# Modulation vectors: one matmul against a table of identities after a block transpose and a VectorE sum, in place of four or eight matmuls against a column of ones

## The reference, cut to what matters

```python
mod = jax.nn.silu(c) @ w_ada[l] + b_ada[l]          # (1, 1024) @ (1024, 6144)
sh1, sc1, g1, sh2, sc2, g2 = jnp.split(mod, 6, axis=-1)
h = modulate(rms_norm(x, norm1_g[l]), sh1, sc1)      # h * (1 + sc1) + sh1
x = x + g1[:, None, :] * token_mixer(h, ...)
h = modulate(rms_norm(x, norm2_g[l]), sh2, sc2)
x = x + g2[:, None, :] * squared_relu_mlp(h, w_ff1[l], w_ff2[l])
```

## Time and profile before

| | |
|---|---|
| median of 3 runs | 3011.77 us (3007.27 to 3013.6) |
| profiled execution, span from first to last instruction | 3012.7 us |
| mean granted TensorE clock | 0.980 |
| PE busy / DVE busy / ACT busy | 2901.2 / 1681.3 / 996.1 us |
| matmuls of the 32 turns (L780) | 448 records |
| DVE additions of the slots (L1930) | 279.6 us busy |

### The profile page before, as it was taken

One profiled execution on the slowest core, in us unless ns is written; L12 is line 12 of the kernel. 1 busy time (PEld: TensorE's weight loads), 2 busy tenths in 40 slices (PEclk: granted clock), 3 DMA queues, 4 the chain that ended last, 5 costly groups with the idle time before them and its releaser, 6 DMA issues.

```text
span 3012.7 us, 39817 instructions
## 1 busy us (share of the span) xinstructions
PE 2901.2 (96%) x15873; PEld 2488.4 (83%) x15873; DVE 1681.3 (56%) x2278; ACT 996.1 (33%) x1374; POOL 117.7 (4%) x156
## 2 busy tenths in 40 slices
PE   6999999999999999999989999999999998999999
PEld 5888887979787888789878888888888987878887
DVE  5656655454555666665487555455555348554444
ACT  3333333232333222332275232122123336432222
POOL 0000000000001100000000000000000000000000
PEclk8999999999999999999989999999999999999999
DMA  6433344535333644333520213222322250222332
GB/s 227 130 118 123 110 148 136 177 109 154 93 119 103 193 129 142 100 111 125 126 54 18 84 43 91 85 88 88 105 78 72 83 112 29 71 73 87 98 104 70
DMA packets 267439, 316.91 MB, mean 105 GB/s; under 512 B 24811, under 2 KB 236155, under 8 KB 267292
## 3 DMA queue, kind: packets, MB, share of 16 engines
q1 hardware_dynamic: 241116, 230.74, 25.1%
q0 software_dynamic: 19456, 72.00, 7.8%
q10 hardware_dynamic: 6720, 12.06, 1.3%
HBM read 291.96 MB, written 11.27 MB: 101 GB/s over the span
## 4 chain that ended last, share of the span: by engine, by line
PE 85%; DVE 6%; ACT 3%; DVEq 3%; issue 2%; DMA 1%; SPq 0%; ACTq 0%
PE psum L611 25%; PE psum L613 24%; PE psum L612 24%; PE psum L1010 2%; PE psum L780 1%; PE psum L826 1%; PE psum L1022 1%; DVE n_t L1863 1%; DVE dneg L2373 1%; DMA ada<-in_w_ada 1%; DVE sba L2384 1%; PE psum L894 1%; DVE w_lo L1875 1%; PE psum L813 1%; ACT pt L1671 1%
## 5 line engine op out<-in xcount | busy, mean ns | idle before, releaser
L611 PE MATMUL psum<-hs_hi,w_hi 128*128 128x512 f32 x1632 | 652.9, 400 | 12.9 <-DVE hs_lo L1867 5.7
L1875 DVE TENSOR_TENSOR w_lo<-raw,w_hi 128x2048 fp32r<-128x2048 f32 (+1 forms) x246 | 435.4, 1770 | 395.9 <-ACT w_hi L1243 283.4
L612 PE MATMUL psum<-hs_hi,w_lo 128*128 128x512 f32 x1632 | 640.1, 392 | 0.0
L613 PE MATMUL psum<-hs_lo,w_hi 128*128 128x512 f32 x1632 | 639.8, 392 | 0.0
L611 PEld LDWEIGHTS psum<-hs_hi,w_hi 128*128 128x128 f32 x1632 | 309.7, 190 | 88.5 <-issue 15.2
L613 PEld LDWEIGHTS psum<-hs_lo,w_hi 128*128 128x128 f32 x1632 | 309.1, 189 | 66.2
L612 PEld LDWEIGHTS psum<-hs_hi,w_lo 128*128 128x128 f32 x1632 | 309.8, 190 | 63.7 <-issue 2.2
L1930 DVE SCALAR_TENSOR_TENSOR ada_acc<-ada_raw,csil,ada_acc 128x512 f32<-128x512 f32 x392 | 279.6, 749 | 48.8 <-DMA ada_raw<-in_w_ada 26.3
L1253 ACT CAST w_hi<-raw 128x2048 fp32r<-128x2048 f32 (+1 forms) x138 | 191.4, 1387 | 328.8 <-PE psum L613 296.0
L611 PE MATMUL psum<-mid_hi,w_hi 128*128 128x512 f32 x768 | 299.7, 390 | 0.0
L612 PE MATMUL psum<-mid_hi,w_lo 128*128 128x512 f32 x768 | 299.2, 390 | 0.0
(11 more groups left out here) (357 smaller groups left out, 4568.2 us busy)
## 6 DMA issues: line engine op xcount, KB each, us to landing
raw<-in_w_in SPq DMA_DIRECT2D x56, 1024.0 KB, 5.2
ada_raw<-in_ada_w POOLq DMA_DIRECT2D x96, 512.0 KB, 4.3
raw<-in_w_ff SPq DMA_DIRECT2D x48, 1024.0 KB, 5.6
raw<-in_w_ff SPq DMA_DIRECT2D x96, 512.0 KB, 3.4
ada_raw<-in_w_ada POOLq DMA_DIRECT2D x32, 512.0 KB, 4.7
raw<-in_w_in SPq DMA_DIRECT2D x24, 512.0 KB, 4.6
ada<-in_w_ada SPq DMA_DIRECT2D x4, 2048.0 KB, 18.6
raw<-in_w_ret_out SPq DMA_DIRECT2D x16, 512.0 KB, 3.5
```

The source lines that it names most:

```text
L611: pe.matmul(dst, lhi, rhi, start=start, stop=False)
L612: pe.matmul(dst, llo, rhi, start=False, stop=False)
L613: return pe.matmul(dst, lhi, rlo, start=False, stop=stop)
L1875: low = dve.tensor_tensor(w_lo[par][:, k0:kt], raw[par][:, k0:kt], w_hi[par][:, k0:kt].bitcast(F32), ALU.subtract)
```

## The change

`ada_acc` is no longer summed over the partitions by PE alone. At the end of the fourth slot of a group DVE transposes the accumulator in square blocks of 32 by 32 (into `ada_raw`, which is free by then) and sums each row of a block, which leaves 16 or 32 numbers on each partition. PE then multiplies them once with `fold`, a 128 by 128 table made of sixteen 32 by 32 identities, which adds the four groups of 32 partitions. The result has the wanted numbers of each quarter of the partitions in columns of its own, so a take now reads and writes 32 partitions at a time: four additions in place of one or two. `fold` is filled once, in the first head, by four copies. It lies where `vrow2` was.

```diff
             def ada_turn(g, par, vecs=1, bank_=C1):
                 pe.wait_ge(ada_sum, 4 * g + 4)
                 ...
-                for v in range(vecs):
-                    for b in range(4):
-                        mm = pe.matmul(bank_[:, 4 * v + b:4 * v + b + 1], ada_acc[par][:, v, b * P:(b + 1) * P], ones_c[:, 0:1],
-                                       start=True, stop=True)
-                mm.then_inc(ada_mm, 1)
+                pe.matmul(bank_[:, 0:16 * vecs], fold[:], ada_acc[par][:, 0, 0:16 * vecs], start=True, stop=True).then_inc(ada_mm, 1)
...
             def ada_slot(s, i=None, two=True):
                 ...
+                if kp == 3:
+                    vecs = 2 if two else 1
+                    turned = ada_raw[par][:, 0:vecs, :].rearrange("p v n -> p (v n)")
+                    dve.drain()
+                    dve.transpose(turned, acc[:, 0:vecs, :].rearrange("p v n -> p (v n)"))
+                    dve.drain()
+                    last = dve.tensor_reduce(acc[:, 0, 0:16 * vecs], turned.rearrange("p (b j) -> p b j", j=32), AX.X, ALU.add)
                 last.then_inc(ada_sum, 1)
 
+            def fold_table():
+                dve.wait_ge(v2_t, 1)
+                for a in range(4):
+                    r_ = slice(32 * a, 32 * a + 32)
+                    dve.tensor_copy(fold[r_, :].rearrange("p (q i) -> p q i", q=4), bc(ident[r_, r_], 4))
+
+            def quarter(bank_, q, vecs):
+                src = bank_[32 * q:32 * q + 32, 0:16 * vecs].rearrange("p (v c q) -> p v c q", v=vecs, q=4)[:, :, :, q]
+                return src if vecs > 1 else src[:, 0]
...
             def ada_take1(g):
                 dve.wait_ge(ada_mm, g + 1)
-                dve.tensor_tensor(mod1[:, bass.ds(16 + 4 * g, 4)], C1[:, 0:4], vec1[:, bass.ds(24 + 4 * g, 4)],
-                                  ALU.add).then_inc(ada_evac, 1)
+                for q in range(4):
+                    r_ = slice(32 * q, 32 * q + 32)
+                    last = dve.tensor_tensor(mod1[r_, bass.ds(16 + 4 * g, 4)], quarter(C1, q, 1), vec1[r_, bass.ds(24 + 4 * g, 4)], ALU.add)
+                last.then_inc(ada_evac, 1)
 
             def ada_take2(g, l):
                 ...
-                for v in range(2):
-                    last = dve.tensor_tensor(mod2[l][:, v, bass.ds(c0, 4)], (X1 if l else C1)[:, 4 * v:4 * v + 4],
-                                             vec2[:, l, bass.ds(c0, 4)], ALU.add)
+                for q in range(4):
+                    r_ = slice(32 * q, 32 * q + 32)
+                    last = dve.tensor_tensor(mod2[l][r_, :, bass.ds(c0, 4)], quarter(X1 if l else C1, q, 2),
+                                             bc(vec2[r_, l, bass.ds(c0, 4)], 2), ALU.add)
                 last.then_inc(ada_evac, 1)
```

More of the change, by code:

```diff
@@ L198, in build @@
         vrow2 = at("vrow2", [P, P], F32, o + 5120)
+        fold = at("fold", [P, P], F32, o + 5120)
         vrow3 = at("vrow3", [V3_ROWS, P], F32, o + 5632)
@@ L2043, in ret_head @@
                     dve.tensor_tensor(qk_raw[:, jb, 0:w], src[:, c0:c0 + w], decay[:, 0:w], ALU.mult).then_inc(s_masked, 1)
+                if not with_out:
+                    fold_table()
                 for s in range(2):
```

## The result

The changed kernel takes 2978.32 us (median of 4 runs, 2972.74 to 2978.58), the kernel before beside it 3011.51 us (3007.27 to 3013.6). That is 33 us less. The ratio of the two is 0.9883, with a 95% interval from 0.987 to 0.9897; 0.9883 of 3011.51 us are 2976.3 us. Forecast were 2987 us and a range from 2977 to 3001.

A forecast was written before the change was run, and what follows sets the result against it. PE, busy 96% of the span, was taken as the bound; 10.1 + 3.5 + 15.4 - 4.1 = 24.9 us off the profiled 3012.7 gave 2987.8, as a median 2987 us, range 2977 to 3001.

The forecast's parts named there:

- Prices of DVE: For 1024 numbers, transpose 1.22 us and sum about 1.22; a take's four additions between 0.36 and about 0.9 us.
- The rivals with a transpose of 2.4 to 6.7 us: Dearer transpose on DVE: two to four times, 2993 to 3006 us (22%), or 6.7 us, 3028 us (4%).
- slower: Rival: transpose at the reciprocal's rate, 6.7 us for 1024 numbers, makes the whole 3028 us; chance 4%.
- A new turn is 0.22 us: On PE, one float32 matmul per turn; saves 0.59 us at turns 0 to 7, 1.48 at 8 to 31.
- Heads: Turns 0 to 5: a loss of 4.1 us, from 0.6, 0.6, 2.3 and 0.6 for a lower-clock stretch.
- The shorter turn in front of L833 starts this chain 0.59 us earlier: Later heads: earlier chain against takes 2 x 0.6 longer, so PE comes out 0.6 us later each.
- D: What a group adds on DVE, transpose, sum and drains: 2.6 us with two vectors, 1.55 with one.
- First feed-forward: Turns 14 to 19: 3.5 us gained, 2.0 at turns 16 to 18, 1.5 at turn 19, none at 14 and 15.
- I count nothing for both: Turns 14 and 15, first feed-forward: no gain, since PE already waits 0.97 us for a weight late to ACT.
- I take half, 0.7 each: Turns 26 and 28, ends of a pass with context: PE idles for its branch, so 0.7 us each, 1.4 together.
- A branch that changes its length: Sign that the forecast is wrong: a loop's branch on PE or DVE changes its length; no size given.
- rival 2: DVE hides everything: up to all 40.2 us come out, 2972 us, more likely half way, 2980; chance 13%.

The follow-up runs named there:

- e3: Changed kernel with each take made as before, one or two additions over 128 partitions (results not the reference's): 2971.52 us.
- e12: Changed kernel without DVE's transpose and sum, takes over 128 partitions, 48 more PE instructions before the first loop (results not the reference's): 2970.40 us.
- e11: The kernel before, unchanged, run once more for a second trace: 3012.71 us.
- e7: The kernel before with 160 more instructions (waits long satisfied) on PE before its first loop: 3001.62 us.
- e8: Changed kernel with a group's four slots in the first feed-forward's loop moved to the first two units of each half pass: 2979.02 us.
- e5: Changed kernel with 48 more instructions (waits long satisfied) on PE before its first loop: 2969.61 us.
- e6: Changed kernel with 256 more instructions (waits long satisfied) on PE before its first loop: 2979.33 us.
- e1_heads_old: Changed kernel with groups 0 to 7 done the old way (one-column matmuls, no transpose or sum, takes of one addition): 2962.09 us.
- e9_fold_late: On e1_heads_old: first feed-forward's transpose and sum placed behind the next weights' low part, turns 13 to 19 one unit or stage later: 2963.01 us.

## Why the forecast came out too small

The sum had 24.9 us, the first traces of the two kernels differ by 36.1. The 11.2 us between them are, by the table: heads -0.9, units 36 to 130 4.2, attention with context -2.2, units 131 to 178 4.9, last layer 5.1. Two steps of the forecast failed on the side of the gain, the half that it took at two ends of a pass with context and the last layer that it left out. One failed on the side of the loss, in the heads. By the medians the miss is 8.3 us (33.2 less 24.9), and still 7.1 with both kernels well placed (32.0). So the place of the code shows which step was wrong, but it doesn't explain the whole miss.

**Prices of DVE: right.** Transpose 1.246 us for 1.22, sum 1.220 for 1.22, the four additions of a take 0.67 us for 0.36 to 0.9, and no new wait of PE for the low part behind unit 131. The rivals with a transpose of 2.4 to 6.7 us, slower among them, fell on the first row.

**The new turn: mis-sized.** "A new turn is 0.22 us" took the pace within a row of matmuls for the price of a single one. It is 0.14, so a turn saves 1.56 and 0.67 us, not 1.48 and 0.59: some 2 us in all.

**Heads: the step "The shorter turn in front of L833 starts this chain 0.59 us earlier" failed.** Forecast was a loss of 4.1 us in turns 0 to 5, measured 5.0. ACT makes `gn_std` after L833's matmul, but not because of it: first it makes `sgate` from a result that PE had before the turn, and then loads a table for 1.28 us. The third head in the kernel before, then in the changed kernel:

```profile
345.77 0.60 ACT L1393 ACTIVATE sgate<-psum 128x512 f32<-128x512 f32 x1 [4.84 <-PE psum L613]
346.38 1.28 ACT L1395 ACT_TABLE_LOAD   x1
347.68 0.69 ACT L1395 ACTIVATE gn_std<-psum,eps_t 128x512 f32<-128x512 f32 x1
```

```profile
349.56 0.60 ACT L1390 ACTIVATE sgate<-psum 128x512 f32<-128x512 f32 x1 [4.84 <-PE psum L614]
350.17 1.28 ACT L1392 ACT_TABLE_LOAD   x1
351.47 0.69 ACT L1392 ACTIVATE gn_std<-psum,eps_t 128x512 f32<-128x512 f32 x1
```

From `sgate` to `gn_std` it is 1.91 us in both, though the `mean_dv` matmul (L833, here L830) starts 0.61 us behind `sgate` in the one and 0.06 us ahead of it in the other. So nearly nothing of the 1.36 us that two turns give comes out. In us from unit 5 to 15, 15 to 25 and 25 to 35: 107.8, 104.5 and 104.5 before; 109.7, 104.4 and 104.4 in e3, whose takes cost what they did; 110.3, 105.8 and 105.8 in the changed kernel. The two later passes lose 1.3 us each where 0.6 was forecast. The first loses 2.5 us where 2.9 was forecast: D costs 1.2 (1.1), the takes 0.6 (1.2), and a stretch of lower clock 1.0 (0.6), and the shorter turns give 0.4 back (e12 beside e11). e7 and e11 have that stretch with before's code, and beside their 401.4 us the changed kernel's 404.7 are a loss of 4.0 in turns 0 to 5. PE waits 4.3 us for `z_lo` there, not over 5.

**First feed-forward: sound, with luck in the first trace.** Turns 16 to 18 saved 0.81 (0.65), turn 15 nothing, as "I count nothing for both" has it, but turn 14 1.13. That is no gain of the change. ACT rounds the weight behind turn 14 as soon as its load has landed, in the kernel before and in e11, which is the same kernel:

```profile
998.08 1.91 ACT L1253 CAST w_hi<-raw 128x2048 fp32r<-128x2048 f32 x1 [8.06 <-DMA raw<-in_w_ff]
```

```profile
997.68 1.91 ACT L1253 CAST w_hi<-raw 128x2048 fp32r<-128x2048 f32 x1 [6.81 <-DMA raw<-in_w_ff]
```

SP issued the load 3.5 us ahead of unit 81 in both, and in both traces of the changed kernel. It landed 6.5 us behind the unit's start in the first trace of before, and 5.2 to 5.4 us in the three others. In e11 PE therefore doesn't wait at turn 14, and the unit takes 9.86 us where it takes 9.84 with the change: nothing is saved, and PE's wait grew from 0 to 1.38 us (the forecast had 2.4, from a trace with the late load). The forecast had also put the late weight on ACT alone; by e8 it hangs on DVE's backlog, which holds back SP's load. Of the 4.2 us that units 36 to 130 gave beyond the forecast, 1.4 are the price of turns 7 to 22 (0.15 at each of 16 to 18 included), 1.1 the late load, and 1.7 stretches of half clock that fell elsewhere. The sum repeats in the second traces with other parts, and which of these 2.8 us belong to the kernels stays open.

**Context stages: the step "I take half, 0.7 each" failed.** The idle time behind turns 26 and 28 was put down to the branch waiting for room in PE's queue. That isn't what it is: it comes and goes with nothing but the place of the code, together with 18 packets of instructions (e5, e6, e7). A branch that changes its length was on the forecast's list of what would make it wrong, but had no price. With the loop well placed in both kernels, e7 to e5, turns 26 and 28 save 1.6 us like the others, and the stage shrinks by 12.7, where eight times 1.56 are 12.5. As timed, the two saved 5.0 us in place of 1.4. That they saved more than 2 x 1.56 goes with a lower clock: in the kernel before 6.8 us at a clock of 0.50 begin in the idle time behind turn 26, in both traces, and in neither trace of the changed kernel:

```profile
1920.60:1927.40 6.80, 5.20 (x12) 4.13 (x13) 4.38 (x7) 0.00 (x0) 0.72 (x1) 0.50 0.30 87
```

```profile
1900.90:1904.40 3.50, 2.12 (x9) 1.44 (x9) 3.43 (x7) 0.00 (x0) 0.00 (x0) 1.00 0.07 9
```

**The last layer: a term that the sum didn't have.** With nothing changed there the profiled execution is 5.1 us shorter. The traces tie it to the clock: both of before are at 750 us, e7 with before's instructions at 744.5, the others at 742.1 to 746.7 and one, e12, at 749.1. Of the 5.1 us, 2.7 lie in one long unit: 191 takes 161.7 and 161.6 us in the two traces of before, 159.0 in both of the changed kernel, and has 17.1 us at half clock in the one and 10.2 in the other. Another 2.7 lie behind the first matmul of the last unit, where second traces differ by 1 us. They give no cause. The kernels reach the place at other times; which of that counts was not separated, and stays open.

The forecast's rival 2, DVE hides everything, isn't what happened, though its time (2972 us, more likely 2980) came close: DVE's part still costs the heads 4.6 us and three ends of a pass 2.3. That the total came that near is luck: 8.7 of the 11.2 us, the two ends of a pass and the last layer, have nothing to do with DVE.

## What to carry to other kernels

Before pricing an edit in a long unrolled loop, look at the queue of instructions and at the branch back: a gap of kind "issue" there may be the code's place, and a few idle instructions in front of the loop can be worth more (9 to 10 us in the medians here, about the same in both kernels) than many an edit, and can fake or hide one. Compare two versions at an equally good place. Before calling an instruction the start of a chain, look at what its reader waits for: L833 stood right ahead of `gn_std`, but a table load set the time. Where an engine with slack takes work over, the gain must be read at each place where it is short: the part of this change in the heads costs 4 us, and the kernel without it (e1_heads_old, 2962 us, which also has the good place) is the fastest that was timed, level with e9_fold_late.

## What the runs showed of the hardware that was not expected

- A loop of 1610 instructions on PE branches back with no idle time, or with 1.7 to 2.4 us of it and a unit behind it that is 1.0 to 1.3 us longer, by its place: 48 instructions more in front of it took 18 packets of 16 KB and 8.7 us of the median away, 256 brought packets and gaps back.
- One float32 matmul of 1, 16 or 32 columns between wide ones costs 0.14 us, each further one 0.223.
- Four additions of 32 partitions each take 0.67 us where one of 128 takes 0.16.
- A weight load that was issued at the same place of the program took 10.0 us in one execution of the kernel before and 8.8 in another, which is a wait of PE of 0.97 us or none.
- The same instructions from unit 130 to unit 131 took 192.9 us in one execution of the changed kernel and 198.6 in another.
